# Two of the eight key tiles of a differential attention multiplied with the values in full fp32 instead of in split fp32r

## The reference

```python
def attend(q_blk):
    s = jnp.einsum('bqhcd,bkhcd->bhcqk', q_blk, k, preferred_element_type=jnp.float32)
    p = jax.nn.softmax(s, axis=-1)
    a = p[:, :, 0] - lam * p[:, :, 1]
    return jnp.einsum('bhqk,bkhe->bqhe', a.astype(v.dtype), v)

o = lax.map(attend, qb)
o = o.transpose(1, 0, 2, 3, 4).reshape(B, S, N_HEADS, V_DIM)
o = rms_norm(o, subln_g) * (1.0 - lambda_init)
return o.reshape(B, S, N_HEADS * V_DIM) @ w_o
```

## Time and profile before

| | |
|---|---|
| median of 3 runs | 2353.82 us (2352.02 to 2357.24) |
| the profiled execution: its own time | 2352.65 us |
| its span in the trace | 2350.9 us |
| granted TensorE clock, mean | 0.997 of full speed |
| TensorE busy | 2303.2 us (98%) |
| VectorE busy | 1399.9 us (60%) |
| ScalarE busy | 992.2 us (42%) |
| GpSimd busy | 1152.9 us (49%) |
| first exponentials of step 0 and step 63 start at | 285.30 and 581.46 us |

### The profile page before, as it was taken

The page is one execution under the profiler, slowest core; times in us unless marked ns, Lnnn a source line. Parts: engine busy times, 40 slices in busy tenths (PEclk is TensorE's granted clock), DMA queues, the critical chain, the costliest instruction groups (busy, mean ns, idle before and its releaser), DMA issues.

```text
span 2350.9 us, 26048 instructions
## 1 busy us (share of the span) xinstructions
PE 2303.2 (98%) x10260; PEld 1870.8 (80%) x10260; DVE 1399.9 (60%) x1311; ACT 992.2 (42%) x1116; POOL 1152.9 (49%) x711
## 2 busy tenths in 40 slices
PE   8999989999999999999999999999999999999997
PEld 6888767777778888888888878887788888888886
DVE  7766899999365555555423654455755555573224
ACT  5211278888444444444212542234544444441122
POOL 2221223333487666674222786653877767632221
PEclk9999999999999999999999999999999999999999
DMA  3634455351322222223422322225222222234222
GB/s 133 224 142 152 162 146 131 92 124 55 126 81 90 81 85 86 81 81 134 162 93 94 114 76 72 78 102 179 72 90 82 86 92 82 81 125 178 94 72 95
DMA packets 79381, 254.23 MB, mean 108 GB/s; under 512 B 8608, under 2 KB 8992, under 8 KB 79264
## 3 DMA queue, kind: packets, MB, share of 16 engines
q1 hardware_dynamic: 79264, 252.63, 32.9%
HBM read 184.44 MB, written 68.16 MB: 107 GB/s over the span
## 4 chain that ended last, share of the span: by engine, by line
PE 73%; issue 13%; DVE 6%; ACT 4%; POOL 2%; DMA 1%; SPq 0%; POOLq 0%; DVEq 0%; ACTq 0%
PE PS L306 23%; PE PS L853 15%; PE PS L855 15%; PE PS L854 15%; DVE nb L1416 2%; POOL Wst L291 2%; PE PS L743 1%; PE PS L764 1%; PE PS L751 1%; PE PS L744 1%; DVE X L1435 1%; ACT X L1084 1%; ACT At L1079 1%; PE PS L773 1%; DVE XB L1463 1%
## 5 line engine op out<-in xcount | busy, mean ns | idle before, releaser
L855 PE MATMUL PS<-XB,U 128*128 128x512 f32 x1556 | 605.4, 389 | 0.0
L853 PE MATMUL PS<-XB,U 128*128 128x512 f32 x1532 | 596.6, 389 | 4.4 <-DVE XB L1463 3.0
L854 PE MATMUL PS<-XB,U 128*128 128x512 f32 x1532 | 596.0, 389 | 0.0
L291 POOL TENSOR_TENSOR Wst<-Wraw,Wst 128x1024 fp32r<-128x1024 f32 (+1 forms) x87 | 208.0, 2392 | 648.7 <-ACT Wst L285 648.7
L306 PE MATMUL PS<-H,Wst 128*128 128x512 f32 x2070 | 470.1, 389 | 0.9 <-POOL Wst L291 0.5
L306 PEld LDWEIGHTS PS<-H,Wst 128*128 128x128 f32 x2070 | 388.4, 188 | 82.4 <-DVE Tv L1559 0.9
L855 PEld LDWEIGHTS PS<-XB,U 128*128 128x128 f32 x1556 | 292.1, 188 | 60.9
L853 PEld LDWEIGHTS PS<-XB,U 128*128 128x128 f32 x1532 | 287.6, 188 | 66.5 <-DVE XB L1463 4.4
L854 PEld LDWEIGHTS PS<-XB,U 128*128 128x128 f32 x1532 | 287.6, 188 | 59.3
L1787 POOL TENSOR_TENSOR U<-U1f,U 128x2048 fp32r<-128x2048 f32 x56 | 260.3, 4649 | 8.2 <-POOL U2f L1761 0.9
L285 ACT ACTIVATE Wst<-Wraw 128x1024 fp32r<-128x1024 f32 (+1 forms) x87 | 88.4, 1019 | 362.7 <-DMA Wraw<-weights 362.7
(11 more groups left out here) (186 smaller groups left out, 3391.0 us busy)
## 6 DMA issues: line engine op xcount, KB each, us to landing
U1f<-ups SPq DMA_DIRECT2D x56, 512.0 KB, 4.6
U2f<-ups SPq DMA_DIRECT2D x56, 512.0 KB, 3.8
Wraw<-weights SPq DMA_DIRECT2D x55, 512.0 KB, 4.1
h_scratch<-Tv SPq DMA_DIRECT2D x47, 512.0 KB, 5.4
Hf<-h_scratch SPq DMA_DIRECT2D x44, 512.0 KB, 4.4
Wraw<-weights SPq DMA_DIRECT2D x32, 448.0 KB, 3.3
x_scratch<-X SPq DMA_DIRECT2D x24, 512.0 KB, 3.2
X<-x_scratch SPq DMA_DIRECT2D x24, 512.0 KB, 7.2
```

The source lines that it names most:

```text
L291: pool.tensor_tensor(w[:, 1, 0:cols], raw[:, 0:cols], w[:, 0, 0:cols].bitcast(F32), ALU.subtract).then_inc(w_lo, 1)
L853: pe.matmul(ps, wh, bh, start=begin, stop=False, skip_group_check=True)
L854: pe.matmul(ps, wh, bl, start=False, stop=False, skip_group_check=True)
L855: ins = pe.matmul(ps, wl, bh, start=False, stop=kp == KP - 1, skip_group_check=True)
```

## The change

Key tiles 6 and 7 (the last 256 keys) are no longer split. `SPLIT_T` is 6; `split_cols` are columns 0 to 767, `whole_cols` columns 768 to 1023.

- The high part of a transposed map is written in two pieces: 768 columns as fp32r, and 256 columns as a plain fp32 copy (`At_whole`, in the same place). The 256-column copy stands first in ScalarE's step, ahead of the first exponential.
- The low part has 768 columns.
- In `values`, tiles 6 and 7 are one fp32 matmul each, in place of three fp32r matmuls each.
- The values are treated in the same way: two ScalarE copies in `v_hi`, a `v_lo` of 768 columns, three stores instead of two, and a shorter second load.

```diff
-            return At[:, b:b + 8, q % 4 * P:(q % 4 + 1) * P]
+            return At[:, b:b + SPLIT_T, q % 4 * P:(q % 4 + 1) * P]
+        def a_whole_tile(q):
+            b = A_HI[q // 4]
+            return At_whole[:, b + SPLIT_T:b + KT, q % 4 * P:(q % 4 + 1) * P]
+        def by_tiles(cols):
+            return slot(2)[:, cols].rearrange("p (t n) -> p t n", n=P)
...
             def load_v(h, parity):
-                for w in range(2):
-                    sp.dma_start(VV[parity][w].bitcast(F32), whole(v_dram[w], h)).then_inc(v_in, 16)
+                sp.dma_start(VV[parity][0].bitcast(F32), whole(v_dram[0], h)).then_inc(v_in, 16)
+                sp.dma_start(VV[parity][1][:, split_cols].bitcast(F32), whole(v_dram[1], h)[:, split_cols]
+                             ).then_inc(v_in, 16)
...
             def transposes(i, q):
                 pe.wait_ge(a_done, i + 1)
                 wait(pe, al_made, i)
+                wait(pe, a_whole, i)
...
                 c = slice(t * P, (t + 1) * P)
-                for w, m in ((0, A_HI), (0, A_LO), (1, A_HI)):
...
+                if t < SPLIT_T:
+                    for w, m in ((0, A_HI), (0, A_LO), (1, A_HI)):
+                        pe.matmul(slot(3)[:, 0:HALF], VV[parity][w][:, c], At[:, m[g] + t, :],
+                                  start=t == 0 and w == 0 and m is A_HI, stop=False)
+                else:
+
+                    pe.wait_ge(a_whole, 4 * u + 4)
+                    ins = pe.matmul(slot(3)[:, 0:HALF], VV[parity][0][:, c].bitcast(F32),
+                                    At_whole[:, A_HI[g] + t, :], start=False, stop=t == KT - 1)
...
             def v_hi(h):
                 act.wait_ge(vt_done, h + 1)
-                wait(act, v_st, h * 32)
-                act.activation(v_hl[0], slot(3), ACT.Copy).then_inc(vh_made, 1)
+                wait(act, v_st, h * 48)
+                act.activation(v_hl[0][:, split_cols], slot(3)[:, split_cols], ACT.Copy).then_inc(vh_made, 1)
+                act.activation(v_whole[:, whole_cols], slot(3)[:, whole_cols], ACT.Copy
+                               ).then_inc(vh_made, 1)
...
             def step(h, ii, tail=False):
                 i = h * QT + ii
+                if lagged(h, ii - 2, tail):
+                    q = (ii - 2) % QT
+                    act.wait_ge(t_done, i - 1)
+                    if q % 4 == 0:
+                        wait(act, pv_done, h * 2 + (ii - 2) // 4 - 1)
+                    act.activation(a_whole_tile(q), by_tiles(whole_cols), ACT.Copy).then_inc(a_whole, 1)
                 if not tail:
                     act.wait_ge(nb_done, 2 * i + 1)
                     wait(act, a_done, i - 1)
...
-                    act.activation(a_tile(A_HI, q), slot(2).rearrange("p (t n) -> p t n", n=P), ACT.Copy
-                                   ).then_inc(ah_made, 1)
+                    act.activation(a_tile(A_HI, q), by_tiles(split_cols), ACT.Copy).then_inc(ah_made, 1)
...
+                    dve.wait_ge(a_whole, i - 1)
                     dve.wait_ge(ah_made, i - 1)
-                    dve.tensor_tensor(a_tile(A_LO, q), slot(2).rearrange("p (t n) -> p t n", n=P),
-                                      a_tile(A_HI, q).bitcast(F32), ALU.subtract).then_inc(al_made, 1)
+                    dve.tensor_tensor(a_tile(A_LO, q), by_tiles(split_cols), a_tile(A_HI, q).bitcast(F32),
+                                      ALU.subtract).then_inc(al_made, 1)
```

More of the change, by code:

```diff
@@ L205, in build @@
         At = at("At", [P, 68, HALF], AR + 32 * K, F32R)
+        At_whole = at("At_whole", [P, 68, HALF], AR + 32 * K)
+        v_whole = at("v_whole", [P, S], AR + (84 + 8) * K)
         A_HI, A_LO = (0, 8), (16, 60)
+        SPLIT_T = KT - 2
+        split_cols, whole_cols = slice(0, SPLIT_T * P), slice(SPLIT_T * P, S)
         on_q = at("on_q", [P, 2, HALF], AR + 80 * K)
@@ L255, in build @@
         inv_done, co_done, a_done, t_done = sem("inverse_done"), sem("coef_done"), sem("a_done"), sem("t_done")
-        ah_made, al_made = sem("ah_made"), sem("al_made")
+        ah_made, al_made, a_whole = sem("ah_made"), sem("al_made"), sem("a_whole_made")
         s0sq_done, dg_done, sqd_done = sem("s0sq_done"), sem("dg_done"), sem("squares_and_eps")
@@ L471, in store_v @@
                 sp.wait_ge(vl_made, h + 1)
-                for w in range(2):
-                    sp.dma_start(whole(v_dram[w], h), v_hl[w].bitcast(F32)).then_inc(v_st, 16)
+                sp.wait_ge(vh_made, 2 * h + 2)
+                sp.dma_start(whole(v_dram[0], h)[:, split_cols], v_hl[0][:, split_cols].bitcast(F32)).then_inc(v_st, 16)
+                sp.dma_start(whole(v_dram[0], h)[:, whole_cols], v_whole[:, whole_cols]).then_inc(v_st, 16)
+                sp.dma_start(whole(v_dram[1], h)[:, split_cols], v_hl[1][:, split_cols].bitcast(F32)
+                             ).then_inc(v_st, 16)
             def store_k(h):
@@ L524, in _ @@
             sp.wait_ge(vt_done, HEADS)
-            sp.wait_ge(v_st, 32)
+            sp.wait_ge(v_st, 48)
             load_v(0, 0)
@@ L540, in load_head @@
                 sp.wait_ge(v_in, 32 * h)
-                sp.wait_ge(v_st, 32 * (h + 1))
+                sp.wait_ge(v_st, 48 * (h + 1))
                 load_v(h, parity)
@@ L698, in v_transpose @@
                 wait(pe, vl_made, h)
+                wait(pe, vh_made, 2 * h)
                 for t in range(KT):
@@ L761, in values @@
                 c = slice(t * P, (t + 1) * P)
-                for w, m in ((0, A_HI), (0, A_LO), (1, A_HI)):
[L763 to L767, removed]
+                if t < SPLIT_T:
[6 more added lines that the diff above has]
+                                    At_whole[:, A_HI[g] + t, :], start=False, stop=t == KT - 1)
+                    if t == KT - 1:
+                        ins.then_inc(pv_done, 1)
             def subln_sum(u):
@@ L798, in step @@
                     pe.wait_ge(vl_made, HEADS)
+                    pe.wait_ge(vh_made, 2 * HEADS)
                 def values_of(half):
@@ L1383, in v_lo @@
             def v_lo(h):
-                dve.wait_ge(vh_made, h + 1)
-                dve.tensor_tensor(v_hl[1], slot(3), v_hl[0].bitcast(F32), ALU.subtract).then_inc(vl_made, 1)
+                dve.wait_ge(vh_made, 2 * h + 2)
+                dve.tensor_tensor(v_hl[1][:, split_cols], slot(3)[:, split_cols], v_hl[0][:, split_cols].bitcast(F32),
+                                  ALU.subtract).then_inc(vl_made, 1)
             def k_lo(h):
```

## The result

| | before | changed |
|---|---|---|
| median | 2352.93 us (4 runs, 2352.02 to 2357.24) | 2407.31 us (4 runs, 2405.53 to 2409.63) |
| span in the trace | 2350.9 us | 2403.7 us |

The account below looks back on a forecast made before the run. It took VectorE to bound the attention before, and a 5.44 us loop of waits after. Start 0.93, 61 such steps and 6.6 for `subln_sum`, less 286.63, added 52.7 us: 2406 us predicted, range 2386 to 2424.

Parts of the forecast that it names:

- The chain of 5.44 us a step: Attention: scores and transposes, small copy, first exponential, high part, second exponential and next scores in a row, 5.44 us a step.
- The steps with `subln_sum`: Thirteen attention steps with both values halves behind the next scores: following scores 0.51 us late each, 6.6 us in all.
- The order on ScalarE: ScalarE's queue is strictly first in, first out, so the first exponential can't pass the waiting small copy; the sum rests on it.
- The fp32 products: In values on TensorE: 0.33 us more in one step of four, nothing in the long step; 5 us if TensorE set the pace.
- Start: Step 2's first exponential now waits for transposes and the small copy: 295.76 instead of 294.83, 0.93 us later.
- The clock: Rival: gaps in TensorE's work lower its clock, 1.8 us a step, 110 us if it lasted, 2516 us; chance 0.05.
- The end: Attention's end: block 62's transposes start some 0.6 us earlier, two groups of values cost 0.66 more; cancelling to 0.
- The sum of 52.7 us: Added time for the whole kernel: 0.93 + 61 x 5.44 + 6.6 - 286.63 us.
- The VectorE saving: Attention: the 768-column low part takes 0.26 us less a step, gaining time only while VectorE sets the step.
- The faster rival: Exponential doesn't wait for the copy in effect; 2338 us by VectorE, about 2348 by TensorE's room; chance 0.04.

Follow-up runs that it names:

- e3_wait_only: Kernel before, with only a ScalarE wait for block i-2's transposes added ahead of step i's first exponential; 2401.09 us, ratio 1.0206.
- e1_copy_behind: Changed kernel with the 256-column copy moved behind the first exponential, directly ahead of the 768-column high part; 2347.48 us, ratio 0.9975.
- e5_values_ahead: Changed kernel with the first half of the values products ahead of scores(i+1, 0) in the subln_sum steps too; 2401.49 us, ratio 1.0203.
- e4_split_first: Kernel before with ScalarE's high part cut in two, 256 columns ahead of the first exponential, no fp32 products, full low part; 2410.88 us, ratio 1.0247.
- e7_three_tiles: e1_copy_behind with three key tiles unsplit in place of two (SPLIT_T = KT - 3); 2346.53 us, ratio 0.9975.
- e9_filled: e4_split_first with three extra fp32r matmuls at each of the two values places in steps 2 to 5; 2404.68 us, ratio 1.0226.

## Why the prediction was right

- **The chain of 5.44 us a step** came out link by link: 2.07, 0.04, 0.28, 1.09, 0.69 and 1.27 us against 2.07, 0.04, 0.27, 1.11, 0.69 and 1.26. e3_wait_only shows that the wait does it, e1_copy_behind that the place does it.
- **The steps with `subln_sum`**, 0.51 late each (its terms, 3.69 - 3.06 - 0.1, give 0.53): in the changed kernel they are by turns 5.91 (479.52 to 485.43, for one) and 6.00 us long against 5.44, on average 0.52 late, 6.8 us in all for the 6.6 of the sum. e5_values_ahead took 5.8 us off.
- **The order on ScalarE**: the prediction had no row with a ready instruction behind a waiting one; the changed kernel has one. The minimum for the exponential of 474.08 had ended at 472.74 (471.52 + 1.22), ScalarE stood idle for 0.64 us until the copy's transposes were done, and the exponential started only behind the copy. The rule that the prediction took from the Trainium skill (TensorE: Matmul & The Clock Gate, the paragraph on engine queue depths; the section Terms, which it names as well, says nothing of queues) agrees with this.
- **The fp32 products** cost nothing in the long step: in the timeline their two records start at 470.93 and take 1.02 us together, as those of L773 did, and the scores behind them start at 471.69, 1.27 after the second exponential, as in the other steps; e4_split_first has none and is no faster.
- **Start**: step 2's exponential came at 295.35, 0.52 later than before, where I had 0.93. The transposes ahead of it ended at 295.04, 0.4 earlier than I had put them. This term was too large by 0.4.
- **The clock**: the rival was right as a mechanism and wrong in extent: it fell in single steps and did not last. I judged the risk by a busy share of 80%, that of the steps with values products. In the first steps there are none, TensorE was busy 2.83 of 5 us, and one step of this trace took 7.02 us: 1.6 us that my sum did not have. The row that I leaned on, 3.44 of 5 us at 1.00, came from steps with shorter gaps (0.57 and 0.81 us, against 1.57 and 0.60).
- **The end**: the first sum of the output projection came at 671.66, 54.08 later than before; the last first exponential was 53.87 later. The end's two terms did cancel, to 0.2. The rest of the program took 1.3 us less than before in these two traces, which no part of the change explains and which lies within what single executions differ.
- The sum of 52.7 us against 52.8 in the spans is therefore better than its parts, and so close by luck: 0.4 too much at the start, 1.6 missing for the clock, 1.3 from elsewhere. The medians lie 54.4 us apart, 1.7 more than the sum.
- **The VectorE saving** (0.26 us a step) was real, and worth nothing in this order. In e1_copy_behind some of it comes through: 0.41 us in four steps, of 1.04 that VectorE gave up. The faster rival's value of 2348 us, made from TensorE's room of 5.4 us, is what e1_copy_behind reached; its condition, that the copy not hold up the exponential, needed an edit. That the value was met does not show TensorE as the bound there: e7_three_tiles, which gives TensorE more work, is no slower.

## What to carry to other kernels

An instruction is priced by what it waits for and by what stands behind it, more than by its length: a copy of 0.38 us that has to wait for the transposes, put ahead of an exponential that had not waited for them, cost 0.87 us in each of 61 steps on average, nearly all of it for the wait, and one place further down it cost none. Before an edit to a written-out order, go once round the loop (each engine's wait, the instruction, the next engine's wait) and compare its length with the busiest engine's work in a step. When the loop is the longer, savings on that engine are worth nothing, and work that fits into the gaps is free, as the fp32 products were here.

## What the runs showed of the hardware that was not expected

TensorE's clock fell in steps that had 8 matmuls and 8 transposes in them and no wait longer than 1.57 us: between the two groups of scores stood 1.57 and 0.60 us of waiting, and from there the clock was at its lower level (1.2 GHz, matmuls of 0.63 us) until the transposes were done or nearly done. Each time cost 1.4 to 1.6 us, and it came in four steps of the trace of e4_split_first, in three of e5_values_ahead and in one of the changed kernel. In the trace of e3_wait_only it came once behind waits of 1.29 and 0.81 us as well (6.65 us against 5.38).

The same waits did not always bring it. In the changed kernel the steps from 295.35 to 311.66 have the same matmuls and the same waits (1.57 and 0.60 us) and took 5.43 to 5.44 us each; one of its stretches there:

```profile
300.00:305.00 5.00, 2.83 (x15) 1.84 (x14) 4.21 (x5) 3.27 (x6) 0.26 (x2) 1.00 1.04 237
```

What decides between them no run here shows. 24 extra matmuls in the gaps of steps 2 to 5 went with the clock at its full level in the trace of e9_filled and made the kernel 6.2 us faster than e4_split_first.

The Trainium skill, in TensorE: Matmul & The Clock Gate, Part 1, says that the lower clock is the default and that activity lifts it. The trace of e9_filled agrees: with more activity, in the same loop of 5.44 us, the clock stayed up.
